# Gate-up weights of experts 5 to 29 loaded in two 64-partition transfers with 32 KB runs

## What is computed

```python
def expert_block(args):
    xblk, e = args
    hgu = xblk @ w_gu[e] + b_gu[e]                 # w_gu[e]: 1024 x 2048, 8 MB
    gate = jnp.minimum(hgu[:, :D_FF], SWIGLU_LIMIT)
    up = jnp.clip(hgu[:, D_FF:], -SWIGLU_LIMIT, SWIGLU_LIMIT)
    act = gate * jax.nn.sigmoid(SWIGLU_ALPHA * gate) * (up + 1)
    return act @ w_down[e] + b_down[e]             # w_down[e]: 1024 x 1024, 4 MB
```

## Time and profile before

| | |
|---|---|
| median of 3 runs | 1092.38 us (1092.22 to 1093.05) |
| profiled execution, span | 1090.9 us, first to last instruction; no time of its own stands beside it |
| PE (TensorE matmul) busy | 1052.1 us, 96% |
| PEld (weight load) busy | 511.6 us |
| DVE (VectorE) busy | 458.4 us |
| ACT (ScalarE) busy | 173.5 us |
| bytes moved by DMA | 432.68 MB, mean 397 GB/s over the span |
| granted TensorE clock, mean | 0.997 of full speed |

### The profile page before, as it was taken

One profiled execution on the slowest core, in us unless ns is written; L12 is line 12 of the kernel. 1 busy time (PEld: TensorE's weight loads), 2 busy tenths in 40 slices (PEclk: granted clock), 3 DMA queues, 4 the chain that ended last, 5 costly groups with the idle time before them and its releaser, 6 DMA issues.

```text
span 1090.9 us, 17307 instructions
## 1 busy us (share of the span) xinstructions
PE 1052.1 (96%) x7085; PEld 511.6 (47%) x7085; DVE 458.4 (42%) x775; ACT 173.5 (16%) x293; POOL 8.9 (1%) x21
## 2 busy tenths in 40 slices
PE   8999999999999999999999999999999999999995
PEld 7999975433333333344334333333343433333332
DVE  5577665333333333333333333333333333323344
ACT  5445533100000000000000000000000000000012
POOL 1000100000000000000000000000000000000000
PEclk9999999999999999999999999999999999999998
DMA  9872899999999999999999999999999999999993
GB/s 302 279 226 105 321 406 373 428 428 426 427 430 427 430 429 427 430 427 430 427 430 429 427 431 427 429 428 429 430 426 431 427 430 429 428 429 425 428 424 152
DMA packets 52480, 432.68 MB, mean 397 GB/s; under 512 B 4629, under 2 KB 21545, under 8 KB 26203
## 3 DMA queue, kind: packets, MB, share of 16 engines
q1 hardware_dynamic: 50817, 430.52, 95.0%
q10 hardware_dynamic: 1634, 1.74, 0.6%
HBM read 431.10 MB, written 1.39 MB: 396 GB/s over the span
## 4 chain that ended last, share of the span: by engine, by line
PE 64%; DMA 28%; DVE 4%; issue 4%; ACT 1%; SPq 1%; DVEq 0%; ACTq 0%
PE PS L1145 23%; PE PS L1174 17%; DMA down_ring<-in_w_down_dram 16%; DMA gu_ring<-in_w_gu_dram 11%; PE PS L913 9%; PE PS L1077 3%; PE PS L1121 2%; PE PS L944 2%; PE PS L1123 1%; PE PS L1188 1%; PE PS L1158 1%; PE PS L1156 1%; DVE pick_twice L1580 1%; PE PS L1192 1%; PE PS L864 0%
## 5 line engine op out<-in xcount | busy, mean ns | idle before, releaser
L1145 PE MATMUL PS<-gu_ring,XgT 128*64 128x512 f32 x2048 | 469.1, 599 | 3.9 <-DMA gu_ring<-in_w_gu_dram 3.9
L1145 PEld LDWEIGHTS PS<-gu_ring,XgT 128*64 128x64 f32 x2048 | 135.1, 136 | 267.1 <-issue 246.4
L1174 PE MATMUL PS<-down_ring,actT 128*64 128x512 f32 x984 | 219.7, 596 | 9.6 <-DMA down_ring<-in_w_down_dram 9.6
L1611 DVE TENSOR_TENSOR Y<-PS,Y 128x1024 f32<-128x1024 f32 (+1 forms) x96 | 117.0, 1220 | 255.1 <-PE PS L1123 255.1
L1174 PEld LDWEIGHTS PS<-down_ring,actT 128*64 128x64 f32 x984 | 67.4, 137 | 137.4 <-issue 118.4
L1642 DVE SCALAR_TENSOR_TENSOR y_low<-PS,slot_gate,y_high 128x512 fp32r<-128x512 f32 x31 | 23.3, 751 | 231.5 <-ACT y_high L800 231.5
L812 ACT ACTIVATE work<-PS 128x512 f32<-128x512 f32 x32 | 19.1, 597 | 456.3 <-PE PS L1145 456.3
L913 PE MATMUL PS<-h_high,win_high 128*128 128x264 f32 (+2 forms) x256 | 71.2, 287 | 0.0
L913 PE MATMUL PS<-h_high,win_low 128*128 128x264 f32 (+2 forms) x256 | 71.0, 286 | 0.0
L913 PE MATMUL PS<-h_low,win_high 128*128 128x264 f32 (+2 forms) x256 | 70.8, 286 | 0.0
L800 ACT ACTIVATE y_high<-PS,slot_gate 128x512 fp32r<-128x512 f32 x31 | 21.3, 687 | 258.3 <-PE PS L1174 258.3
(11 more groups left out here) (235 smaller groups left out, 778.3 us busy)
## 6 DMA issues: line engine op xcount, KB each, us to landing
gu_ring<-in_w_gu_dram SPq DMA_DIRECT2D x119, 2048.0 KB, 28.5
down_ring<-in_w_down_dram SPq DMA_DIRECT2D x60, 2048.0 KB, 21.9
gu_ring<-in_w_gu_dram SPq DMA_DIRECT2D x18, 1024.0 KB, 10.0
gu_ring<-in_w_in_dram SPq DMA_DIRECT2D x16, 1024.0 KB, 8.8
gu_ring<-in_w_down_dram SPq DMA_DIRECT2D x4, 1024.0 KB, 28.0
down_ring<-in_w_down_dram SPq DMA_DIRECT2D x3, 1024.0 KB, 10.6
down_ring<-in_w_pool_up_dram SPq DMA_DIRECT2D x1, 2048.0 KB, 11.4
gu_ring<-in_w_conv_out_dram SPq DMA_DIRECT2D x2, 1024.0 KB, 6.2
```

What stands on the lines that cost most here:

```text
L1145: last = mm(PS[SLOTS * h:SLOTS * h + SLOTS, b, :], XgT[:, k, :], w[:, D * b + HALF * h:D * b + HALF * h + HALF], start=(k == 0), stop=(k = ...
L1174: last = mm(PS[SLOTS * h:SLOTS * h + SLOTS, bank, :], acts[:, f % 4, f // 4, :], rows[:, f, HALF * h:HALF * h + HALF], start=(f == 0), sto ...
L1611: tt(Y[rows, t, :].rearrange("p (h n) -> p h n", h=2), PS[rows, bank:bank + 2, :], Y[rows, t, :].rearrange("p (h n) -> p h n", h=2), ALU.a ...
```

## The change

For experts 5 to 29, an expert's gate-up weights come by *halves* (512 rows, 4 slots) in place of pairs. Rows are now dealt four to a partition (r = 4), so a partition's run in a half is 32 KB. A half is brought by two loads, `load_long(e, parity, h, q)` with q = 0 and 1: the first fills partitions 0 to 63 of the four slots, the second partitions 64 to 127, each 2 MB. SP waits once ahead of a half, until all four slots are free, in place of once ahead of each pair. For the experts before 5 and for the last two (30 and 31), `load_gu` and `load_row` stay, with 128 partitions; with r = 4 they read every other 16 KB (or every fourth 8 KB) of the rows. The last loop of SP is one pair of items shorter, and experts 30 and 31 stand behind it with `item_gu`. The order of gate-up and down loads stays as it was.

PE now waits for both semaphores of a half ahead of k = 0 and of k = 4. It waits by pairs, as before, for experts 0, 1, 30 and 31 (`by_pairs=True`).

```diff
             def load_gu(e, parity, m):
-                src = w_gu[0, bass.ds(e, 1), 2 * P * m:2 * P * m + 2 * P, :].rearrange("a (p r) n -> (a p) (r n)", r=2)
+                h, q = divmod(m, 2)
+                src = w_gu[0, bass.ds(e, 1), HALF * h:HALF * h + HALF, :].rearrange("a (p q r) n -> (a p) q (r n)", q=2, r=2)
                 sp.dma_start(gu_ring[:, KT * parity + 2 * m:KT * parity + 2 * m + 2, :].rearrange("p s n -> p (s n)"),
-                             src).then_inc(gu_landed[CH * parity + m], 16)
+                             src[:, q, :]).then_inc(gu_landed[CH * parity + m], 16)
+
+            def load_long(e, parity, h, q):
+                rows = slice(HALF * h + 2 * P * q, HALF * h + 2 * P * q + 2 * P)
+                src = w_gu[0, bass.ds(e, 1), rows, :].rearrange("a (p r) n -> (a p) (r n)", r=CH)
+                sp.dma_start(gu_ring[SLOTS * q:SLOTS * q + SLOTS, KT * parity + CH * h:KT * parity + CH * h + CH, :
+                                     ].rearrange("p s n -> p (s n)"), src).then_inc(gu_landed[CH * parity + 2 * h + q], 16)
...
+            def item_long(i, e, parity, halves=range(2)):
+                for h in halves:
+                    sp.wait_ge(gu_used, 8 * i + (4 * h - 12))
+                    for q in range(2):
+                        load_long(e, parity, h, q)
+
...
-                item_gu(i + 2, e2, 1)
+                item_long(i + 2, e2, 1)
                 item_down(i, i)
-                item_gu(i + 3, e3, 0)
+                item_long(i + 3, e3, 0)
                 item_down(i + 1, e1)
...
-            def gate_up(i, u, landed, two_before, bias=None):
+            def gate_up(i, u, landed, two_before, bias=None, by_pairs=False):
...
-                    if k % 2 == 0:
-                        by_row = 16 if k == 0 and u == 0 and two_before is not None else 0
-                        pe.wait_ge(gu_landed[CH * u + k // 2], landed + by_row)
+                    for m in ((k // 2,) if k % 2 == 0 else ()) if by_pairs else ((k // 2, k // 2 + 1) if k % CH == 0 else ()):
+                        by_row = 16 if m == 0 and u == 0 and two_before is not None else 0
+                        pe.wait_ge(gu_landed[CH * u + m], landed + by_row)
```

More of the change, by code:

```diff
@@ L488, in _ @@
                 e3 = sp.snap(2 * pair + 6)
-                item_gu(i + 2, e2, 1)
+                item_long(i + 2, e2, 1)
                 item_down(i, i)
-                item_gu(i + 3, e3, 0)
+                item_long(i + 3, e3, 0)
                 item_down(i + 1, e1)
-            first, second = (0, 1), (2, 3)
+            first, second = (0,), (1,)
             i = 2 * AHEAD + 1
-            item_gu(i + 2, i + 2, 1, first)
+            item_long(i + 2, i + 2, 1, first)
             item_down(i, i)
@@ L501, in _ @@
                 e3 = sp.snap(2 * pair + (2 * AHEAD + 5))
-                item_gu(i + 1, e1, 1, second)
-                item_gu(i + 2, e2, 0, first)
+                item_long(i + 1, e1, 1, second)
+                item_long(i + 2, e2, 0, first)
                 item_down(i, i)
-                item_gu(i + 2, e2, 0, second)
-                item_gu(i + 3, e3, 1, first)
+                item_long(i + 2, e2, 0, second)
+                item_long(i + 3, e3, 1, first)
                 item_down(i + 1, e1)
             i = 2 * AHEAD + 2 * HALVED + 2
-            item_gu(i + 1, i + 1, 1, second)
+            item_long(i + 1, i + 1, 1, second)
             item_down(i, i)
-            with sp.Fori(0, E // 2 - 2 - AHEAD - HALVED) as pair:
+            with sp.Fori(0, E // 2 - 3 - AHEAD - HALVED) as pair:
                 i = sp.snap(2 * pair + (2 * AHEAD + 2 * HALVED + 3))
@@ L880, in turn_small_rows @@
                 nc.tensor.transpose(PS[:, 4, 8:24], param_rows, ident[0:16, 0:16])
-                by_r = gffn_rows.rearrange("m (p r) -> m r p", r=2)
-                for q in range(2):
-                    last = nc.tensor.transpose(PS[:, 4, 24:32].rearrange("p (m r) -> p r m", r=2)[:, q, :], by_r[:, q, :],
-                                               ident[0:CH, 0:CH])
+                by_r = gffn_rows.rearrange("m (p r) -> m r p", r=CH)
+                for q in range(CH):
+                    last = nc.tensor.transpose(PS[:, 4, 24:32].rearrange("p (m r) -> p r m", r=CH)[:, q, :], by_r[:, q, :],
+                                               ident[0:2, 0:2])
                 last.then_inc(rows_turned, 1)
@@ L986, in by_row @@
             def by_row(rows, t, k):
[L987 to L988 removed]
+                m, q = divmod(k, CH)
+                return Y[0:rows, t, HALF * m:HALF * m + HALF].rearrange("t (p r) -> t r p", r=CH)[:, q, :]
             def turn_samples():
@@ L1193, in turn, with item @@
                 last.then_inc(up_turned, 1)
-            def item(i, u, landed, before=None, two_before=None, bias=None):
-                gate_up(i, u, landed, two_before, bias)
+            def item(i, u, landed, before=None, two_before=None, bias=None, by_pairs=False):
+                gate_up(i, u, landed, two_before, bias, by_pairs)
                 if before is not None:
@@ L1203, in item @@
                 turn(i)
-            gate_up(0, 0, 32, None)
+            gate_up(0, 0, 32, None, by_pairs=True)
             turn_gates()
@@ L1227, in _ @@
             item(two_before, 1, more * (8 * E) + 8 * E, from_end(4), from_end(5), bias=1)
-            item(before, 0, landed, two_before, from_end(4), bias=2)
-            gate_up(last, 1, landed, two_before)
+            item(before, 0, landed, two_before, from_end(4), bias=2, by_pairs=True)
+            gate_up(last, 1, landed, two_before, by_pairs=True)
             way_back(before)
```

30 lines of the change are left out of this document (16 added, 14 removed).

## The result

The changed kernel takes 1779.94 us (median of five runs, 1763.70 to 1832.06); the kernel before, run beside it, takes 1092.22 (1091.66 to 1093.05). The ratio is 1.622, with a 95% interval from 1.619 to 1.625; it compares the fastest runs alone, since the time of the changed kernel itself varies by 4% from run to run. The profiled execution is the longest of the five, so what is counted in it adds up to 1832 and not to 1780.

What follows compares the result with a forecast made beforehand. The prediction took the stream of DMA loads to bound the kernel: 100 long loads at 4.68 us more each, 468 us, with waits and tail at 0, take it to 1560 us; near-full collisions (0.56) ranged from 1500 to 1640.

Steps and rivals of the forecast that it cites:

- two narrow windows of the earlier trace: Moments with 32-partition `b_gu` and `b_down` loads, where packets took 1.86 to 1.95 times as long; basis for the long-load price.
- Down loads (128 partitions) stay at 4.895: In the expert stream, each unchanged down load was to keep its 4.895 us.
- the 48.1 us for an expert: Load stream per changed expert: four gate-up loads at 9.57 us plus two down loads at 4.895, in place of 29.4.
- the engines don't run dry: 0: At SP's wait for four slots, 13 us of issued work was to remain queued, so no cost.
- Waits: SP's and PE's waits by halves: PE's second-half start 4.9 us later, made up before the end; cost 0.
- 468, 0 and 0: Loads 100 x 4.68 = 468 us more, SP's waits 0, and the tail behind the last gate-up landing unchanged, 0.
- Partly out of step: Rival for the 100 long loads: engines with a lead avoid part of the collisions; 1302 us, chance 0.20.
- Its own counter-argument: Against that rival: a load counts as landed only when its slowest engine is done; no size given.
- its 1.8 us of slack an expert: PE's spare time against the loads, claimed to make up its later starts, 1.8 us per expert.
- No collisions, and PE's later starts cost: Rival: second halves start 4.9 us later and reach the end; 1093 us (0.08), or a little more, 1097 (0.03).
- TensorE's clock: Rival on PE: half clock all the time adds 178 us; expected hidden behind loads; no separate chance given.
- if the share of the DMA engines falls while loads are slow (then it is SP's waits that starve them): A stated sign of error in the profile after; the prediction expected the engines' share to stay near 1.

Runs made afterwards that it cites:

- wide32: The changed kernel with each half brought by one 4 MB load on 128 partitions with 32 KB runs; 1095.13 us, ratio 1.0025.
- across_in_step: The changed kernel with halves loaded as partitions 32 to 95, 0 to 31, 96 to 127, and SP's down loads waiting for the third load; 1444.90 us.
- in_step: The changed kernel with SP also waiting, ahead of each expert's down loads, until its last long load has landed; 1701.75 us, ratio 1.5556.
- narrow16: The changed kernel, still 64 partitions a load, with two 16 KB runs per partition instead of one of 32 KB; 1635.18 us, rerun 1633.99 to 1818.99.
- wide16: The changed kernel with its waits and row dealing, but each half by two loads of 128 partitions with 16 KB runs; 1098.52 us, ratio 1.005.
- deal4: Only the change's dealing of four rows to a partition kept; loads and waits by pairs as in the kernel before; 1094.06 us, ratio 1.0013.
- wide32_to_27: wide32 with experts 28 to 31 loaded and waited for by pairs; 1094.56 us, ratio 1.0011.
- light: The changed kernel with six of eight products of the up half of each gate-up left out on PE; 1814.88 us.
- narrow16_in_step: narrow16 with SP also waiting, ahead of each expert's down loads, for its last gate-up load to land; 1695.44 us, ratio 1.5497.

## Why the prediction was right in kind and wrong in size

**Right: 64 partitions of one side of 64 come in at half rate.** The prediction priced a long load at 9.57 us. In the trace of the changed kernel the first ones land at 273.1, 283.1, 293.1 and 303.2 us: 10.0 each. A 32 KB packet takes 2.5 us, where it takes 1.22 in wide32 with engines equally busy. The two narrow windows of the earlier trace rows were the right rows, and a little too kind. 10.0 in place of 9.57 is 43 us over 100 loads. One inference from them was looser than it sounds: the row doesn't show which of the four `b_gu` loads its 45 packets belong to (58 packets of 2 KB had passed between 11.4 and 12.2 us already), so that two loads of one side were in the window together was a guess, which the experiments bear out. The page "SBUF — State Buffer" of the Trainium skill, section "Door 1: The DMA port swizzle", divides partitions by bit 6 of their number, which is this side of 64; across_in_step agrees with this rule, for packets of 32 KB pass there at full speed (43% of its 32 KB packets took under 1.3 us, and the 2 MB on 32 to 95 are half of them; in_step has none).

**The step that failed: "Down loads (128 partitions) stay at 4.895".** From it came the 48.1 us for an expert. From the landing of the last gate-up load ahead to that of the second down load it is 9.8 us in the kernel before. In the profiled execution of the changed kernel it is 22.6 us on average from 600 to 1600 us (9.6 to 25.2), while the gate-up loads, at 9.1 us each, come in a little faster than 10.0. Down loads nearly stay only while the engines are in step. Then an expert takes 50.5 (narrow16): 39.7 for four gate-up loads, and 10.8 for two down loads. With 21.1 us more for each of 25 experts that is +528, and such an execution takes 1634 to 1635, inside the stated range. No run of the changed kernel was that fast; its profiled execution is in step only up to some 400 us. Counted from the packet records (long packets: how many, share under 1.3 us, mean ns; 16 KB packets: how many, mean ns; engines busy of 16):

```
kernel         window us | 32 KB packets    | 16 KB packets | busy | GB/s
wide32          540: 840 | 2660, 1.00, 1217 |  2572,   615  | 16.1 | 431
after           273: 410 |  677, 0.00, 2499 |   714,   678  | 16.1 | 247
after           600:1600 | 4316, 0.01, 2513 |  4594,   832  | 14.7 | 217
in_step         600:1600 | 4736, 0.00, 2493 |  4964,   667  | 15.2 | 237
across_in_step  400:1300 | 5294, 0.43, 1847 |  5474,   664  | 15.0 | 292
```

An expert gives each engine 16 packets of 32 KB and 16 of 16 KB. Early in the changed kernel that is 16 x 2.50 + 16 x 0.68 = 50.9 us of work. Later it is 16 x 2.51 + 16 x 0.83 = 53.5 us, in engines of which 14.7 / 16 = 0.92 are busy: 58.2 us, and 12.58 million bytes at 217 GB/s are 58.0. So drift costs 7 us an expert in two parts. 2.6 us are slower packets of down loads, which pass while other engines are on a long load (the windows at 1046.50 and 1062.20 above). The larger part, 4.7 us, is idle engines. This contradicts a second term, "the engines don't run dry: 0" under *Waits*: slots come free by the slowest engine, and SP's wait for them lets the queue run empty for the engines that are ahead. Counted from SP's issues and the landings, from 600 to 1600 us the time from an engine's end on one load to SP's issue of the next adds up to 1.0 idle engine of sixteen. The share says 1.3 to 1.4 (14.7 where 16.1 are busy in the kernel in step); the rest isn't told apart, but an issued load takes time to begin (1.0 us from 1066.91). In the kernel before and in narrow16 the same count gives 0. That the lag stops growing at 40 to 50 us fits this limit.

**The sum.** The last gate-up load lands at 1781.7 in the profiled execution, 1053.4 before: +728. In narrow16 it is 1585.8: +532, the half rate alone. The difference, 196 us, is drift (about 145 in the median run, 1780 less 1635). Behind that landing 48.5 us follow, against the 37.5 of the earlier trace rows: +11 (narrow16 has 47.6 there). The chain from 1750 us on has PE and no load in it, so PE is behind the loads at the end here as well. Together +739, the difference of the spans. The prediction had 468, 0 and 0.

**A rival with its sign wrong.** "Partly out of step" had engines that lead take out collisions, at 1302 us. Drift came, and cost time: of the long packets of the changed kernel 1% took under 1.3 us. Its own counter-argument ("the one pair of engines without a lead sets the pace") was the better half: a load lands with its slowest engine.

**Waits, priced at 0.** wide16 less deal4 says 4.5 us. The prediction had PE make it up. In the profiled wide16, the slowest of its five executions, 42.3 us are behind the landing of the last gate-up load instead of 37.5. (That landing is at 1057.2 instead of 1053.4, but the loads were 3.6 us late at 206 us already, in an execution whose clock fell to 0.83 from 165 to 185 us; between there and the end the stream lost 0.2 us, so the prediction was right that the queue doesn't run dry by the new waits alone.) In the kernel before PE waits for that load and starts 8 products; in wide16 the chain from 1050.10 has nothing but PE in it:

```profile
1050.10 5.30 PE PS L1161 x24
...
1056.07 3.58 PE PS L1161 x16
...
1060.32 3.58 PE PS L1161 x16
```

PE is behind the loads at the end, although experts 30 and 31 go by pairs. In wide32_to_27, where 28 and 29 do so too, 40.5 us are still behind the landing, so its 1.8 us of slack an expert don't bring PE back as the prediction had it; why not is open. The 4.9 us that the rival "No collisions, and PE's later starts cost" charged was about right in size, and hidden in 688 us here.

**TensorE's clock.** It fell, to 0.824 on average, with PE busy 65% of the span. The prediction expected it hidden behind the loads; light, with a still lower clock and less work, fits that. The condition named for being wrong, "if the share of the DMA engines falls while loads are slow (then it is SP's waits that starve them)", came true in part: the share is 0.87 to 0.90 in the windows from 500 us on, and it is SP's waits.

**Open.** What sets off the first lag, and in narrow16 in some executions only. The records don't say which partitions an engine writes at a given time. Other ways to keep engines in step (waits less often than once an expert, the two halves on two queues) weren't tried.

## What to carry to other kernels

Split a stream of loads along a partition's run or by rows, not into partitions 0 to 63 and 64 to 127: here each such load came in at half rate, even with its sister right behind it in the queue; if one must be narrower than 128, lay it across 64 (32 to 95 was tried). Where a DMA-bound kernel's time scatters by several per cent, look at how far apart the engines land a load: the slowest one sets the landing, holds the slots, and starves the others, and an added wait can then make the kernel faster. The loads that lose the time needn't be those that were changed. An effect seen in one run of such a kernel may be luck; run it again before building on it.

## What the runs showed of the hardware that was not expected

- Loads on one side of 64 let single engines of the sixteen fall up to 50 us behind in the same queue, and they fall behind at the 128-partition loads in between; with loads of 128 partitions alone the distance is 2.8 to 3.0 us for 800 us. The same kernel ran in 1634 and in 1819 us, without and with it.
- A wait that lets every engine finish once an expert costs 60 us in all (narrow16 and narrow16_in_step) and takes the scatter from 4% (the changed kernel) to 0.4% (in_step).
- An engine on a load of 128 partitions takes 1.8 to 1.9 us for a packet of 16 KB while the others are on one-sided loads, in place of 0.61; alone, it takes 1.21 us for a one-sided packet of 32 KB, in place of 2.5 (the changed kernel, 1046 to 1068 us).
- A load of 64 partitions on 32 to 95 has packets of 32 KB in 1.2 us, full speed, where one on 0 to 63 has them in 2.5. The Trainium skill says in "SBUF — State Buffer", section "Can I just issue two DMAs to hit both halves?", that only a transfer over all 128 partitions reaches all 16 ports; the full speed on 32 to 95, and 1444.90 us of across_in_step against 1701.75 of in_step, speak against "only".
- 32 KB runs on 128 partitions gain 0.16 us an expert (29.21 for 29.37), 40 ns for each 2 MB, or some 10 ns for each packet less on an engine, by an estimate that puts all of it down to the packets.
